# A two-layer decoder trunk on one core: layer 1's weighted sums of values as three fp32r passes instead of one fp32 matmul

## The chip, the cores and the metric

The kernel runs on one core of a Trainium2 chip. The metric is the device time of one execution in microseconds. The core has a matmul engine (TensorE, PE in the profile; its weight loads are PEld), a vector engine (VectorE, DVE), a scalar engine (ScalarE, ACT), GpSimd (POOL) and an engine that issues transfers (SyncE, SP). The engines run side by side, each through its own instructions in order, and wait for each other on semaphores.

## The reference

A sequence of 256 tokens of width 2048 goes through two layers. Each has a mixer and a squared-ReLU MLP, with RMS norms around both. Layer 0's mixer is a gated unit beside a dilated attention. Layer 1's mixer, which the change touches, is stick-breaking attention with 16 heads of 128:

```python
def block(args):
    qblk, start = args
    z = jnp.einsum('bhqe,bhke->bhqk', qblk, k).astype(jnp.float32)
    qpos = start + jnp.arange(ATT_BLOCK)
    causal = kpos[None, :] < qpos[:, None]
    log_1m_beta = jnp.where(causal, jax.nn.log_sigmoid(-z), 0.0)
    rev = lax.cumsum(log_1m_beta, axis=3, reverse=True)
    excl = jnp.concatenate([rev[..., 1:], jnp.zeros_like(rev[..., :1])], axis=-1)
    a = jnp.where(causal, jnp.exp(jax.nn.log_sigmoid(z) + excl), 0.0)
    return jnp.einsum('bhqk,bhke->bhqe', a.astype(v.dtype), v)
```

The last line, the weighted sum of the values, is what the change computes in another way.

## The kernel before

All large products are projections of 256 tokens by weights that stream in from memory. A *unit* is one projection of 256 tokens to 512 columns over a depth of 2048. It is cut into 8 *ticks*. A tick covers a depth of 256, so 2 blocks of 128, for 2 blocks of 128 tokens. To keep fp32 accuracy at the rate of fp32r, each fp32 operand is split into a high part (rounded to fp32r) and a low part (the rest), and a tick makes three matmuls for each block: high by high, high by low and low by high, 12 matmuls of 512 columns in all (`tick_tokens`).

The weights of a tick are split just in time. ACT writes `w_hi` (`conv`, L381) and DVE subtracts to get `w_lo` (`conv`, L711). A ring of four ticks holds them, so ACT may write the slot of tick t + 4 once PE has finished tick t. On ACT and DVE the work for tick t + 4 is issued at step t (`conv_at`).

Everything else is hung on these steps as `extras`, a table from a step number to a list of functions. On ACT and DVE the functions of step t are issued ahead of the split of tick t + 4. On PE they are issued ahead of the matmuls of tick t. What is issued where is therefore written out by hand, and on each engine it is done in that order.

Layer 1's input projection is done in four groups of four heads, 3 units (24 ticks) each: q, k and v (`qkv_group`). The attention of group g runs in the extras of the 24 ticks of group g + 1 (`l1_extras`), and that of the last group in the extras of the output projection (`out_phase`, whose ticks are counted the same way). For one group the old order is:

- PE: scores at step 0, the suffix sums of heads 0 and 1 at step 8 and of heads 2 and 3 at step 12 (`l1_suffix`), the values at step 15 (`l1_values`).
- ACT: logarithms at 1 and 3, high part of the softplus at 4 and 9 (`l1_soft_hi`, L538), the exponential that gives the weights at 10 and 13 (`l1_weights`, L543), high part of the output at 15 (`o_hi`, L516).
- DVE: softplus at 3 and 6, its low part at 6 and 10 (`l1_soft_lo`, L937), the exponent at 9 and 12 (`l1_exponent`, L932), low part of the output at 15 (`o_lo`, L911). DVE also turns q and k from token-major to head-major in 32x32 blocks (`turn`, L818): q at steps 9 to 14 with 2, 2, 4, 2, 4, 2 instructions (`TURNS_L1`), k at steps 17 to 20 with 4 each. The output phase has no such turns.

For one head, `values` computes 256 output columns from the first 128 keys and 128 more from the second 128 keys, both as plain fp32 matmuls:

```python
mm(ps[:, 6 + b, i * T:(i + 1) * T], v_sb[:, 0, vh], w[:, i, 0:T], i == 0, False)
last = mm(ps[:, 6 + b, i * T + P:(i + 1) * T], v_sb[:, 1, vh], w[:, i, T:TRI], False, True)
```

In the output phase the ticks that use the output of the last four heads are the ones at positions 18 and 19 (and later ones), and PE waits there for the low parts of these heads (`ready` in `out_phase`, on `s_olo`).

Of the kernel before, what the change touches and what calls it, by code (L numbers as in the profile page):

```python
# [29 lines left out]
F32 = mybir.dt.float32  # L30
F32R = mybir.dt.float32r
ALU = mybir.AluOpType
ACT = mybir.ActivationFunctionType
AX = mybir.AxisListType

P = 128
T = 256
TB = T // P
D = 2048
KT = D // P  # L40
# [13 lines left out]
HG = 4  # L54
# [5 lines left out]
TRI = 3 * P  # L60
# [40 lines left out]
def trunk_kernel(nc, x_in, pre_mix, post_mix, pre_ffn, post_ffn, ab_w_in, ln_g, ln_b, sgu_w, sgu_b,  # L101
                 ab_w_out, sb_w_in, sb_w_out, ffn_w1, ffn_w2, shapes, out):
    ctx = ExitStack()
    with ctx:  # L104
        def sb(name, shape, dt=F32):
            return ctx.enter_context(nc.sbuf_tensor(name, shape, dt))

        def sem(name):
            return ctx.enter_context(nc.semaphore(name))
# [4 lines left out]
        hid_hi = sb("hid_hi", [P, KT, T], F32R)  # L114
        hid_lo = sb("hid_lo", [P, KT, T], F32R)
# [8 lines left out]
        v_sb = sb("v_sb", [P, TB, NC])  # L124
        soft_hi = sb("soft_hi", [P, 2, TRI], F32R)
        soft_lo = sb("soft_lo", [P, 2, TRI], F32R)
        sum_mats = sb("sum_mats", [P, 2 * P], F32R)
        zs = sb("zs", [P, HG, TRI])
# [12 lines left out]
        ps = ctx.enter_context(nc.psum_tensor("ps", [P, 8, 512], F32))  # L141
# [11 lines left out]
        gain_rows = tmp[0:4 * KT, HG - 1, 0:P]  # L153
        q_flat, k_flat = (t[:, :, :].rearrange("p h t -> p (h t)").rearrange("p (b n) -> p b n", b=TB)
                          for t in (qT, kT))
        relu_tok, sq_tok, sq_T = q_flat, k_flat, qT
        q_tok, k_tok = k_flat, y_sb[:, 0, 0:T * HG].rearrange("p (b n) -> p b n", b=TB)
        junk = tmp[:, 0:HG, :].rearrange("p h c -> p (h c)")
# [52 lines left out]

        s_mix, s_sgt, s_gate, s_ghi, s_glo = (sem(n) for n in ("s_mix", "s_sgt", "s_gate", "s_ghi", "s_glo"))
        s_turned = sem("s_turned")
        s_sc = sem("s_sc")
        s_zs = sem("s_zs")
        s_sm = sem("s_sm")
# [11 lines left out]
        s_a = sem("s_a")  # L228
        s_o = sem("s_o")
# [141 lines left out]
        def _(act):  # L371
# [142 lines left out]
            def o_hi(n, b, tile):  # L514
                act.wait_ge(s_o, n + 1)
                nc.scalar.activation(hid_hi[:, bass.ds(tile, 2), :],  # L516
                                     ps[:, 6 + b, :].rearrange("p (h t) -> p h t", t=T), ACT.Copy).then_inc(s_ohi, 1)
# [6 lines left out]
            def l1_logs(b, grp):  # L524
                pair = 2 * grp + b
                z, t = zs[:, 2 * b:2 * b + 2, :], tmp[:, 2 * b:2 * b + 2, :]
                act.wait_ge(s_zs, 4 * grp + (L0_HEADS + 2 * b + 2))
                nc.scalar.activation(t, z, ACT.Abs).then_inc(s_ab, 1)
                act.wait_ge(s_ab, 3 * pair + 1)
                nc.scalar.activation(t, t, ACT.Exp, scale=-1.0).then_inc(s_ab, 1)  # L530
                act.wait_ge(s_ab, 3 * pair + 2)
                nc.scalar.activation(t, t, ACT.Ln, bias=1.0).then_inc(s_ab, 1)

            def l1_soft_hi(b, grp):
                act.wait_ge(s_sp, 2 * grp + (b + 1))
                if b == 1:
                    act.wait_ge(s_S, 2 * grp + 1)
                nc.scalar.activation(soft_hi[:, :, :], tmp[:, 2 * b:2 * b + 2, :], ACT.Copy).then_inc(s_sphi, 1)  # L538

            def l1_weights(b, grp):  # L540
                z = zs[:, 2 * b:2 * b + 2, :]
                act.wait_ge(s_e, 2 * grp + (b + 1))
                nc.scalar.activation(z, z, ACT.Exp).then_inc(s_a, 1)  # L543

            def l1_extras(grp):
                return {1: [lambda: l1_logs(0, grp)], 3: [lambda: l1_logs(1, grp)], 4: [lambda: l1_soft_hi(0, grp)],
                        9: [lambda: l1_soft_hi(1, grp)], 10: [lambda: l1_weights(0, grp)],
                        13: [lambda: l1_weights(1, grp)],
                        15: [lambda: o_hi(2 * grp + 4, 0, 4 * grp), lambda: o_hi(2 * grp + 5, 1, 4 * grp + 2)]}

            def qkv_group(u, extras):
                for i in range(3):
# [138 lines left out]
            for g in range(1, L1_GROUPS):  # L691
                qkv_group(U_IN1 + 3 * g, l1_extras(g - 1))
            out_phase(U_OUT1, l1_extras(L1_GROUPS - 1), 3)
            ffn(U_FFN1, 1)


        @block.vector
        def _(dve):
# [210 lines left out]
            def o_lo(n, b, tile):  # L909
                dve.wait_ge(s_ohi, n + 1)  # L910
                nc.vector.tensor_tensor(hid_lo[:, bass.ds(tile, 2), :], ps[:, 6 + b, :].rearrange("p (h t) -> p h t", t=T),  # L911
                                        hid_hi[:, bass.ds(tile, 2), :].bitcast(F32), ALU.subtract).then_inc(s_olo, 1)
# [11 lines left out]
            def l1_softplus(b, grp):  # L924
                dve.wait_ge(s_ab, 6 * grp + 3 * b + 3)
                t = tmp[:, 2 * b:2 * b + 2, :]
                nc.vector.scalar_tensor_tensor(t, zs[:, 2 * b:2 * b + 2, :], 0.0, t, ALU.max, ALU.add).then_inc(s_sp, 1)

            def l1_exponent(b, grp):
                dve.wait_ge(s_S, 2 * grp + (b + 1))  # L930
                for z, sums in ((zs[:, 2 * b:2 * b + 2, 0:T], ps[:, 6, :]), (zs[:, 2 * b:2 * b + 2, T:TRI], ps[:, 7, 0:T])):
                    last = nc.vector.tensor_tensor(z, z, sums.rearrange("p (h t) -> p h t", h=2), ALU.add)  # L932
                last.then_inc(s_e, 1)

            def l1_soft_lo(b, grp):
                dve.wait_ge(s_sphi, 2 * grp + (b + 1))
                nc.vector.tensor_tensor(soft_lo[:, :, :], tmp[:, 2 * b:2 * b + 2, :], soft_hi[:, :, :].bitcast(F32), ALU.subtract  # L937
                                        ).then_inc(s_splo, 1)

            def l1_extras(grp):  # L940
                return {3: [lambda: l1_softplus(0, grp)], 6: [lambda: l1_softplus(1, grp), lambda: l1_soft_lo(0, grp)],
                        9: [lambda: l1_exponent(0, grp)], 10: [lambda: l1_soft_lo(1, grp)],
                        12: [lambda: l1_exponent(1, grp)],
                        15: [lambda: o_lo(2 * grp + 4, 0, 4 * grp), lambda: o_lo(2 * grp + 5, 1, 4 * grp + 2)]}

            def qkv_group(u, extras, q_plan, scores):
                def scaled(i, dst, factor=None):
# [132 lines left out]
            for i in range(2):  # L1080
                last = nc.vector.tensor_scalar(act_hi[:, i, :], ps[:, X_BANK[0], i * T:(i + 1) * T], gpre[:, i:i + 1], None,  # L1081
                                               ALU.mult)
# [76 lines left out]
        def _(pe):  # L1159
            def mm(dst, lhsT, rhs, start, stop):  # L1160
                return nc.tensor.matmul(dst, lhsT, rhs, start=start, stop=stop, skip_group_check=True)  # L1161
# [230 lines left out]
            def values(b, w):  # L1392

                for i in range(2):
                    vh = slice((2 * b + i) * P, (2 * b + i + 1) * P)
                    mm(ps[:, 6 + b, i * T:(i + 1) * T], v_sb[:, 0, vh], w[:, i, 0:T], i == 0, False)
                    last = mm(ps[:, 6 + b, i * T + P:(i + 1) * T], v_sb[:, 1, vh], w[:, i, T:TRI], False, True)
                last.then_inc(s_o, 1)
# [9 lines left out]
            def l1_scores(grp):  # L1408

                pe.wait_ge(s_turned, grp + 3)  # L1410
                pe.wait_ge(s_olo, 2 * grp + 4)
                for h in range(HG):
                    mm(ps[:, 4 + h, 0:T], kT[:, h, 0:P], qT[:, h, :], True, True)
                    mm(ps[:, 4 + h, T:TRI], kT[:, h, P:T], qT[:, h, P:T], True, True).then_inc(s_sc, 1)

            def l1_suffix(b, grp):

                pe.wait_ge(s_splo, 2 * grp + (b + 1))
                pe.wait_ge(s_sums, 1)
                pe.wait_ge(s_zs, 4 * grp + (L0_HEADS + 4))  # L1420
                if b == 1:
                    pe.wait_ge(s_e, 2 * grp + 1)
                early = ps[:, 6, :]
                early_q1 = early.rearrange("p (h t) -> p h t", h=2)[:, :, P:T]
                late = ps[:, 7, 0:T]
                suffix_r, ones_r = sum_mats[:, 0:P], sum_mats[:, P:2 * P]
                for z, first in ((soft_hi, True), (soft_lo, False)):
                    mm(early, suffix_r, z[:, :, 0:T], first, False)
                    mm(early_q1, ones_r, z[:, :, T:TRI], False, not first)
                    last = mm(late, suffix_r, z[:, :, T:TRI], first, not first)  # L1430
                last.then_inc(s_S, 1)

            def l1_values(grp):
                pe.wait_ge(s_a, 2 * grp + 2)
                for b in range(2):
                    values(b, zs[:, 2 * b:2 * b + 2, :])

            def l1_extras(grp):
                return {0: [lambda: l1_scores(grp)], 8: [lambda: l1_suffix(0, grp)], 12: [lambda: l1_suffix(1, grp)],
                        15: [lambda: l1_values(grp)]}  # L1440

            def qkv_group(u, extras, fresh=None):
                for i in range(3):
# [130 lines left out]
```

## Time and profile before

| | |
|---|---|
| time, median of 3 runs | 2127.61 us (2127.42 to 2128.24) |
| the profiled execution | 2127.44 us, span of its trace 2125.6 us |
| TensorE clock granted over the span | 0.999 of full speed |
| PE busy | 2114.7 us, 99% |
| DVE busy | 1474.8 us, 69% |
| ACT busy | 1029.1 us, 48% |
| DMA | 406.81 MB, queue q1 at 58.0% of 16 engines' span |

A busy share is the time in which an engine had an instruction under way, over the whole span. It is an average over stages with different limits. Layer 1's attention lies between 1052 and 1415 us. There a tick takes 2.72 us when nothing else is on PE, which is the distance between ACT's splits of weights.

### The profile page before, as it was taken

The numbers are of one execution on the slowest core, as the hardware profiler recorded it, in microseconds if no ns is written. First come the engines' busy times: TensorE is split into PE (matmuls) and PEld (weight loads), VectorE is DVE, ScalarE is ACT, GpSimd is POOL, SyncE is SP. The second block draws the span as 40 slices with busy tenths as digits, with TensorE's granted clock in tenths as the row PEclk, the third lists the DMA queues.
The fourth block names the chain that finished last, engine by engine and source line by source line (L and its number), as shares of the span: only waits on it lengthen the run. The fifth ranks groups of instructions, "written<-read, shape, count | busy, mean of one in ns | idle before, by whom it ended". The sixth has DMA issues, their size and how long they took to land.

```text
span 2125.6 us, 25468 instructions
## 1 busy us (share of the span) xinstructions
PE 2114.7 (99%) x9470; PEld 1751.6 (82%) x9470; DVE 1474.8 (69%) x1902; ACT 1029.1 (48%) x1183; POOL 18.3 (1%) x24
## 2 busy tenths in 40 slices
PE   9999999999999999999999999999999999999998
PEld 7888888888888888888888888888888888888886
DVE  5797857864775775686778778577756856764875
ACT  6444445543543453454645554665434534544543
POOL 0000000000000000000000000000000000000000
PEclk9999999999999999999999999999999999999999
DMA  9655555656655656655555555456556566656553
GB/s 321 208 177 167 192 197 160 204 193 195 198 194 187 186 205 214 183 197 198 174 183 178 178 172 204 160 159 217 195 187 193 180 212 181 198 196 217 179 200 117
DMA packets 204077, 406.81 MB, mean 191 GB/s; under 512 B 6544, under 2 KB 9936, under 8 KB 203472
## 3 DMA queue, kind: packets, MB, share of 16 engines
q1 hardware_dynamic: 203856, 405.50, 58.0%
q8 instruction: 63, 1.03, 0.2%
q14 instruction: 30, 0.25, 0.0%
q10 hardware_dynamic: 128, 0.03, 0.0%
HBM read 403.41 MB, written 2.10 MB: 191 GB/s over the span
## 4 chain that ended last, share of the span: by engine, by line
PE 99%; DVE 1%; issue 0%; POOL 0%; ACT 0%; POOLq 0%; DVEq 0%
PE ps L1161 98%; PE ps L1304 1%; DVE x_sb L755 0%; PE ps L1388 0%; DVE tmp L1044 0%; POOL rst L351 0%; ACT tmp L483 0%; PE ps L1509 0%; DVE w_lo L711 0%; POOLq L104 0%; DVE act_pair L1081 0%; DVE act_pair L761 0%; DVE y_sb L1051 0%; DVEq L104 0%; DVE w_lo L789 0%
## 5 line engine op out<-in xcount | busy, mean ns | idle before, releaser
L711 DVE TENSOR_TENSOR w_lo<-w_raw,w_hi 128x1024 fp32r<-128x1024 f32 x750 | 910.4, 1225 | 573.2 <-ACT w_hi L381 570.1
L381 ACT ACTIVATE w_hi<-w_raw 128x1024 fp32r<-128x1024 f32 x750 | 789.0, 1060 | 898.2 <-PE ps L1161 894.1
L1161 PE MATMUL ps<-w_hi,act_pair 128*128 128x512 f32 x3456 | 1072.5, 390 | 0.7 <-DVE act_pair L1081 0.6
L1161 PEld LDWEIGHTS ps<-w_hi,act_pair 128*128 128x128 f32 x3456 | 647.2, 188 | 136.8 <-issue 2.2
L1161 PE MATMUL ps<-w_lo,act_pair 128*128 128x512 f32 x1728 | 670.3, 390 | 0.0
L1161 PE MATMUL ps<-w_hi,hid_hi 128*128 128x512 f32 x1280 | 498.8, 390 | 0.0
L1161 PE MATMUL ps<-w_hi,hid_lo 128*128 128x512 f32 x1280 | 498.1, 389 | 0.0
L1161 PE MATMUL ps<-w_lo,hid_hi 128*128 128x512 f32 x1280 | 498.0, 389 | 0.0
L1161 PEld LDWEIGHTS ps<-w_lo,act_pair 128*128 128x128 f32 x1728 | 324.1, 188 | 66.3 <-DVE w_lo L789 0.3
L818 DVE STREAM_TRANSPOSE qT<-kT 32x256 f32<-32x256 f32 x608 | 265.0, 436 | 42.0 <-ACT kT L593 32.7
L1161 PEld LDWEIGHTS ps<-w_lo,hid_hi 128*128 128x128 f32 x1280 | 240.3, 188 | 49.7
L1161 PEld LDWEIGHTS ps<-w_hi,hid_lo 128*128 128x128 f32 x1280 | 240.3, 188 | 49.7
L1161 PEld LDWEIGHTS ps<-w_hi,hid_hi 128*128 128x128 f32 x1280 | 240.3, 188 | 49.6
L598 ACT ACTIVATE hid_hi<-qT 128x512 fp32r<-128x512 f32 x64 | 36.9, 625 | 123.8 <-DVE qT L818 123.8
L818 DVE STREAM_TRANSPOSE kT<-y_sb 32x256 f32<-32x256 f32 x96 | 41.8, 436 | 1.6
L1009 DVE TENSOR_TENSOR hid_lo<-qT,hid_hi 128x512 fp32r<-128x512 f32 x64 | 41.2, 685 | 0.0
L589 ACT ACTIVATE qT<-ps,rst 128x512 f32<-128x512 f32 x64 | 40.0, 675 | 0.0
L593 ACT ACTIVATE kT<-qT 128x1024 f32<-128x1024 f32 x32 | 33.9, 1060 | 1.0
L412 ACT ACTIVATE act_pair<-ps,gpre 128x256 fp32r<-128x256 f32 (+1 forms) x80 | 28.7, 448 | 9.7 <-PE ps L1304 9.7
L761 DVE SCALAR_TENSOR_TENSOR act_pair<-ps,gpre,act_pair 128x256 fp32r<-128x256 f32 (+1 forms) x70 | 28.7, 456 | 2.7 <-ACT act_pair L412 2.5
L1023 DVE TENSOR_TENSOR y_sb<-y_sb,ps 128x1024 f32<-128x1024 f32 x24 | 29.2, 1216 | 0.0
L351 POOL TENSOR_TENSOR rst<-rst,neg_half 128x1 f32<-128x1 f32 (+1 forms) x13 | 9.4, 719 | 2100.2 <-DVE rst L845 2004.9
(104 smaller groups left out, 460.0 us busy)
## 6 DMA issues: line engine op xcount, KB each, us to landing
w_raw<-in_ffn_w_dram SPq DMA_DIRECT2D x256, 1024.0 KB, 5.3
w_raw<-in_sb_w_in_dram SPq DMA_DIRECT2D x48, 1024.0 KB, 5.1
w_raw<-in_ab_w_in_dram SPq DMA_DIRECT2D x36, 1024.0 KB, 5.1
w_raw<-in_ab_w_out_dram SPq DMA_DIRECT2D x16, 1024.0 KB, 5.0
w_raw<-in_sb_w_out_dram SPq DMA_DIRECT2D x16, 1024.0 KB, 5.0
w_raw<-in_ab_w_in_dram SPq DMA_DIRECT2D x6, 512.0 KB, 8.8
x_sb<-in_x_dram SPq DMA_DIRECT2D x8, 256.0 KB, 7.4
gpost<-in_norm_post_mix_dram SPq DMA_DIRECT2D x2, 1024.0 KB, 7.5
```

The costliest lines, as they stand in the source:

```text
L381: nc.scalar.activation(w_hi[:, t % RING, :, :], w_raw[:, t // 2, h:h + 2, :], ACT.Copy).then_inc(hi_ready, 1)
L412: last = nc.scalar.activation(act_hi[:, kt, part], ps[:, X_BANK[j], i * T + part.start:i * T + part.stop], ACT.Copy, scale=gpre[:, k * KT ...
L589: last = nc.scalar.activation(relu_tok[:, b, :], ps[:, 2 * (j % 2) + b, :], ACT.Relu, scale=rst[:, 6 + b:7 + b])
L593: nc.scalar.activation(sq_tok, relu_tok, ACT.Square).then_inc(f_sq, 1)
L598: nc.scalar.activation(hid_hi[:, 4 * j + i:4 * j + i + 2, :], sq_T[:, i:i + 2, :], ACT.Copy).then_inc(f_hi, 1)
L711: nc.vector.tensor_tensor(w_lo[:, t % RING, :, :], w_raw[:, t // 2, h:h + 2, :], w_hi[:, t % RING, :, :].bitcast(F32), ALU.subtract).then_ ...
L761: last = nc.vector.scalar_tensor_tensor(act_lo[:, kt, part], ps[:, X_BANK[j], i * T + part.start:i * T + part.stop], gpre[:, k * KT + kt:k ...
L818: last = nc.vector.transpose(cols[:, :, :, tp, :], rows[:, :, :, fq, :])
L1009: nc.vector.tensor_tensor(hid_lo[:, tiles, :], sq_T[:, i:i + 2, :], hid_hi[:, tiles, :].bitcast(F32), ALU.subtract).then_inc(done, 1)
L1023: nc.vector.tensor_tensor(ys, ys, bank2(j % 2), ALU.add).then_inc(post_done, 1)
L1161: return nc.tensor.matmul(dst, lhsT, rhs, start=start, stop=stop, skip_group_check=True)
L1304: last = nc.tensor.transpose(ps[:, X_BANK[j], i * T + b * P:i * T + (b + 1) * P], x_sb[:, b, kt * P:(kt + 1) * P], ident)
```

## The change

Layer 1's `l1_values` no longer calls `values`. The 256 columns over the first 128 keys become three fp32r matmuls (v high by weights high, v high by weights low, v low by weights high), and the 128 columns over the second 128 keys stay one fp32 matmul. For this ACT writes the high part of the weights (512 columns for each two heads, right behind the exponential) and of v (512 columns for four heads), and DVE the low parts. The buffers are ones that are free then: the last four tiles of `hid_hi` and `hid_lo` for the weights, `soft_hi` and `soft_lo` for v. PE's values move from step 15 to 16 and wait for the low parts. `o_hi` and `o_lo` move from step 15 to 17. DVE's new steps are 13 (low part of the first two heads' weights) and 15 (of the other two's, and v's). Layer 0 keeps `values`.

```diff
@@ -541,12 +549,17 @@
                 act.wait_ge(s_e, 2 * grp + (b + 1))
                 nc.scalar.activation(z, z, ACT.Exp).then_inc(s_a, 1)
+                act.wait_ge(s_a, 2 * grp + (b + 1))
+                nc.scalar.activation(wide_hi[:, 2 * b:2 * b + 2, :], z[:, :, 0:T], ACT.Copy).then_inc(s_a_hi, 1)
+
+            def l1_v_high(grp):
+                nc.scalar.activation(half_hi, v_first, ACT.Copy).then_inc(s_v_hi, 1)
 
             def l1_extras(grp):
                 return {1: [lambda: l1_logs(0, grp)], 3: [lambda: l1_logs(1, grp)], 4: [lambda: l1_soft_hi(0, grp)],
                         9: [lambda: l1_soft_hi(1, grp)], 10: [lambda: l1_weights(0, grp)],
-                        13: [lambda: l1_weights(1, grp)],
-                        15: [lambda: o_hi(2 * grp + 4, 0, 4 * grp), lambda: o_hi(2 * grp + 5, 1, 4 * grp + 2)]}
+                        13: [lambda: l1_weights(1, grp)], 14: [lambda: l1_v_high(grp)],
+                        17: [lambda: o_hi(2 * grp + 4, 0, 4 * grp), lambda: o_hi(2 * grp + 5, 1, 4 * grp + 2)]}
@@ -937,11 +950,21 @@
+            def l1_weights_low(b, grp):
+                dve.wait_ge(s_a_hi, 2 * grp + (b + 1))
+                nc.vector.tensor_tensor(wide_lo[:, 2 * b:2 * b + 2, :], zs[:, 2 * b:2 * b + 2, 0:T],
+                                        wide_hi[:, 2 * b:2 * b + 2, :].bitcast(F32), ALU.subtract).then_inc(s_a_lo, 1)
+
+            def l1_v_low(grp):
+                dve.wait_ge(s_v_hi, grp + 1)
+                nc.vector.tensor_tensor(half_lo, v_first, half_hi.bitcast(F32), ALU.subtract).then_inc(s_v_lo, 1)
+
             def l1_extras(grp):
                 return {3: [lambda: l1_softplus(0, grp)], 6: [lambda: l1_softplus(1, grp), lambda: l1_soft_lo(0, grp)],
                         9: [lambda: l1_exponent(0, grp)], 10: [lambda: l1_soft_lo(1, grp)],
-                        12: [lambda: l1_exponent(1, grp)],
-                        15: [lambda: o_lo(2 * grp + 4, 0, 4 * grp), lambda: o_lo(2 * grp + 5, 1, 4 * grp + 2)]}
+                        12: [lambda: l1_exponent(1, grp)], 13: [lambda: l1_weights_low(0, grp)],
+                        15: [lambda: l1_weights_low(1, grp), lambda: l1_v_low(grp)],
+                        17: [lambda: o_lo(2 * grp + 4, 0, 4 * grp), lambda: o_lo(2 * grp + 5, 1, 4 * grp + 2)]}
@@ -1432,12 +1455,21 @@
             def l1_values(grp):
                 pe.wait_ge(s_a, 2 * grp + 2)
+                pe.wait_ge(s_a_lo, 2 * grp + 2)
+                pe.wait_ge(s_v_lo, grp + 1)
                 for b in range(2):
-                    values(b, zs[:, 2 * b:2 * b + 2, :])
+                    for i in range(2):
+                        h = 2 * b + i
+                        dst = ps[:, 6 + b, i * T:(i + 1) * T]
+                        mm(dst, half_hi[:, h, :], wide_hi[:, h, :], i == 0, False)
+                        mm(dst, half_hi[:, h, :], wide_lo[:, h, :], False, False)
+                        mm(dst, half_lo[:, h, :], wide_hi[:, h, :], False, False)
+                        last = mm(dst[:, P:T], v_sb[:, 1, h * P:(h + 1) * P], zs[:, h, T:TRI], False, True)
+                    last.then_inc(s_o, 1)
 
             def l1_extras(grp):
                 return {0: [lambda: l1_scores(grp)], 8: [lambda: l1_suffix(0, grp)], 12: [lambda: l1_suffix(1, grp)],
-                        15: [lambda: l1_values(grp)]}
+                        16: [lambda: l1_values(grp)]}
```

## Rows read from the trace of the kernel before

**Rows 1.** The page: PE's share of the span, and the chain that ended last.
```profile
PE 2114.7 (99%) x9470; PEld 1751.6 (82%) x9470; DVE 1474.8 (69%) x1902; ACT 1029.1 (48%) x1183; POOL 18.3 (1%) x24
PE 99%; DVE 1%; issue 0%; POOL 0%; ACT 0%; POOLq 0%; DVEq 0%
```
**Rows 2.** The chain in order of time (start, us, what), layer 1's attention.
```profile
1052.52 362.24 PE ps L1161 x1646
```
**Rows 3.** Waits of 1050 to 1415 us: us in total, times, longest.
```profile
ACT w_hi L381 <- PE ps L1161: 161.3, 94, 4.3
```
**Rows 4.** Timeline (start, us, instruction) of PE around the first group's values.
```profile
1149.66 2.78 PE L1161 MATMUL ps<-zs,v_sb 128*128 128x256 f32 x16
1152.19 0.48 PE L1161 MATMUL ps<-w_hi,act_pair 128*128 128x512 f32 x1
1152.51 0.40 PE L1161 MATMUL ps<-w_lo,act_pair 128*128 128x512 f32 x1
```
**Rows 5.** Timeline of PE, the suffix sums in fp32r: 512, 256 and 256 columns, twice.
```profile
1140.54 0.62 PE L1161 MATMUL ps<-soft_hi,sum_mats 128*128 128x512 f32 x3
1140.99 0.64 PE L1161 MATMUL ps<-soft_lo,sum_mats 128*128 128x512 f32 x3
1141.46 0.40 PE L1161 MATMUL ps<-w_hi,act_pair 128*128 128x512 f32 x1
```
**Rows 6.** Timeline of DVE in the first group, steps 10 to 15.
```profile
1139.78 1.23 DVE L711 TENSOR_TENSOR w_lo<-w_raw,w_hi 128x1024 fp32r<-128x1024 f32 x1
...
1150.23 0.89 DVE L818 STREAM_TRANSPOSE qT<-kT 32x256 f32<-32x256 f32 x2
1151.14 1.23 DVE L711 TENSOR_TENSOR w_lo<-w_raw,w_hi 128x1024 fp32r<-128x1024 f32 x1
1152.28 1.51 DVE L911 TENSOR_TENSOR hid_lo<-ps,hid_hi 128x512 fp32r<-128x512 f32 x2
1156.36 1.23 DVE L711 TENSOR_TENSOR w_lo<-w_raw,w_hi 128x1024 fp32r<-128x1024 f32 x1 [2.57 <-ACT w_hi L381]
```
**Rows 7.** Timeline of ACT in the same stretch.
```profile
1137.73 0.85 ACT L543 ACTIVATE zs<-zs 128x768 f32<-128x768 f32 x1
1138.48 1.04 ACT L381 ACTIVATE w_hi<-w_raw 128x1024 fp32r<-128x1024 f32 x1
...
1145.44 0.83 ACT L543 ACTIVATE zs<-zs 128x768 f32<-128x768 f32 x1
1147.19 1.06 ACT L381 ACTIVATE w_hi<-w_raw 128x1024 fp32r<-128x1024 f32 x1 [0.93 <-PE ps L1161]
```
**Rows 8.** Groups of 1125 to 1197 us: count, busy us, mean ns, idle before.
```profile
L911 DVE TENSOR_TENSOR hid_lo<-ps,hid_hi 128x512 fp32r<-128x512 f32 x2 | 1.4, 688 | 0.1
L516 ACT ACTIVATE hid_hi<-ps 128x512 fp32r<-128x512 f32 x2 | 1.2, 597 | 0.9 <-PE ps L1161 0.9
```
**Rows 9.** Timeline of DVE, step 14's split in the other two groups.
```profile
1223.62 1.23 DVE L711 TENSOR_TENSOR w_lo<-w_raw,w_hi 128x1024 fp32r<-128x1024 f32 x1
1296.08 1.23 DVE L711 TENSOR_TENSOR w_lo<-w_raw,w_hi 128x1024 fp32r<-128x1024 f32 x1
```
**Rows 10.** Timeline of ACT and DVE in the output phase, splits of steps 14, 15, 16.
```profile
1367.33 1.06 ACT L381 ACTIVATE w_hi<-w_raw 128x1024 fp32r<-128x1024 f32 x1 [1.66 <-PE ps L1161]
...
1368.42 1.23 DVE L711 TENSOR_TENSOR w_lo<-w_raw,w_hi 128x1024 fp32r<-128x1024 f32 x1 [1.49 <-ACT w_hi L381]
...
1373.78 1.23 DVE L711 TENSOR_TENSOR w_lo<-w_raw,w_hi 128x1024 fp32r<-128x1024 f32 x1 [2.57 <-ACT w_hi L381]
1376.50 1.23 DVE L711 TENSOR_TENSOR w_lo<-w_raw,w_hi 128x1024 fp32r<-128x1024 f32 x1 [1.50 <-ACT w_hi L381]
```
**Rows 11.** All waits of PE in the whole execution: us in total, times, longest.
```profile
PE ps L1161 <- POOL rs_bc L337: 1.2, 1, 1.2
PE ps L1161 <- DVE act_pair L1081: 0.6, 1, 0.6
```
**Rows 12.** The first 12 us: length, PE, PEld, DVE, ACT, POOL busy, PEclk.
```profile
0.00:12.00 12.00, 10.17 (x42) 7.45 (x43) 5.03 (x10) 5.34 (x11) 0.98 (x8) 1.00 0.80 271
```

More of the change, by code:

```diff
@@ L155, in trunk_kernel @@
                           for t in (qT, kT))
+        wide_hi, wide_lo = (t[:, KT - HG:KT, :] for t in (hid_hi, hid_lo))
+        half_hi, half_lo = (t[:, :, :].rearrange("p c n -> p (c n)")[:, 0:HG * P].rearrange("p (h t) -> p h t", t=P)
+                            for t in (soft_hi, soft_lo))
+        v_first = v_sb[:, 0, :].rearrange("p (h c) -> p h c", c=P)
         relu_tok, sq_tok, sq_T = q_flat, k_flat, qT
@@ L213, in trunk_kernel @@
         s_turned = sem("s_turned")
+        s_a_hi = sem("s_a_hi")
+        s_a_lo = sem("s_a_lo")
+        s_v_hi = sem("s_v_hi")
+        s_v_lo = sem("s_v_lo")
         s_sc = sem("s_sc")
```

## The prediction

> **What bounds the kernel now.** I first read the page for the engine that is busy and on the chain that ended last. PE has 99% of both [rows 1]. So the sum of what PE does is the time, and time that ACT or DVE spend matters only where PE stands still for it. The chain in order of time then shows whether PE stands still in the stretch that is changed: it runs through layer 1's whole attention without a break, 362.24 us in one piece [rows 2]. The waits of that stretch hold none of PE on an engine; the largest, 161.3 us in 94 pieces, is ACT waiting for PE [rows 3]. Layer 1's attention is therefore hidden behind the projections today, except for its own matmuls. Two questions decide the change: how much PE time it takes off the values, and whether the new operands are ready when PE comes to ask for them. The second needs DVE's timeline, because a DVE that is 75% busy over a stretch can still be behind at the one step that matters.
>
> **The matmuls themselves.** The eight fp32 matmuls of one group of heads appear as 16 records from 1149.66 to 1152.19, 2.53 us, and the first matmul behind them takes 0.32 instead of 0.23 us, so 0.09 more [rows 4]. By columns that is 4 x (256 + 128) = 1536 columns in 2.53 us. The 256-column part is two thirds of it, 1.69 us, 0.42 each; the 128-column part 0.84, 0.21 each. The new 256-column part is 12 fp32r matmuls. No row has that mix, but the suffix sums are near: two of 512 and four of 256 columns take 1141.46 - 1140.54 = 0.92 us [rows 5]. With 2 x 0.2267 for the wide ones (a tick of 12 takes 2.72 [rows 10]) the four narrow ones take 0.47, 0.117 each. Twelve make 1.40 us against 1.69: 0.29 us less for a group of heads, 1.2 us less for four. Bounds: if each of the three new changes from fp32 back to fp32r in a group costs 0.09, as the one behind the values does today, the gain is 0.02 a group, nothing; if a 256-column pass costs just half of a 512-column one, 0.113, it is 0.33 a group, 1.3 us. I take 1.2, because the suffix sums are the same kind of instruction with changing weights.
>
> The Trainium skill (FP8 and Floating Point Precision, TensorE Precision Notes) says that true fp32 takes four passes through the array. Three passes instead of four would give back a quarter of 1.69 us, 0.42 a group and 1.7 us in all; the fp32r rows give less, and I go by them. The rule is in any case a bound on what the change can bring: under 0.1% of the run.
>
> **What ACT gets.** Two copies of 512 columns behind the exponentials and one for v, 0.60 us each [rows 8]. At step 13 the exponential ends at 1146.27 and the next split, which waits for PE, starts at 1147.19, so the copy fits in between; at step 14 ACT idles 1.66 us ahead of a split in the same rhythm [rows 10]. These two cost nothing; without that cover they would cost DVE's next split 0.6 us, as at step 10. At step 10 there is no idle time: the exponential ends at 1138.58 and its split overlaps it [rows 7]. The copy starts at about 1138.61, the split at 1139.13 instead of 1138.48 and ends at 1140.17, and DVE, which takes it up at 1139.78 today [rows 6], can do so at 1140.22. DVE is 0.45 us later.
>
> **What DVE gets, and who waits.** From 1139.78 to 1153.79 DVE has no idle time at all: its rows from step 10 to step 15 follow each other with no releaser noted, down to the first gap, 2.57 us, ahead of 1156.36 [rows 6]. So the 0.45 us of step 10 is still there at step 15. At step 13 it gets one subtraction of 512 columns. The nearest row is the output's low part, 688 ns [rows 8]; instructions that follow each other overlap by 0.09, so it adds 0.60. Queued behind it are four turns and the split of tick 17, which have slack of their own. Step 14's split started at 1151.14 and now starts at 1152.19. Step 15's two subtractions follow it, at 1153.33 and 1153.93, and end at 1154.62.
>
> PE's step 16 waits for the second one. Without the values at step 15, tick 15 starts at 1149.66 and ends 2.72 us later, at 1152.38. With some 0.05 for the semaphore PE stands still from 1152.38 to 1154.67, **2.3 us**. Nothing behind it on PE can go ahead: the whole stream is one queue. The other two groups inside the projection have the same rows, shifted by 72.5 us (step 14's split at 1223.62 and 1296.08 [rows 9]), so 3 x 2.3 = 6.9 us. Bounds for one of these: 1.7 if the copy at step 10 delays nothing and the subtractions overlap more, 2.9 if each costs its whole 0.69 and the copies on ACT 0.7.
>
> In the output phase there are no turns, and DVE keeps up: its split at step 14 runs at 1368.42, paced by ACT, which is paced by PE [rows 10]. The two subtractions start at 1369.56 and 1370.16 and end at 1370.85. Tick 15 would end at 1369.8 (ACT's 1367.33, less 0.25 from PE's last matmul to ACT, plus 2.72). PE stands 1.1 us here, even with no backlog, because a split on ACT and DVE ends 2.5 us after the tick that frees its slot, and the next tick is over after 2.72.
>
> One more wait comes from the output's move to step 17. In the output phase PE needs the low parts of the last heads at tick 18. ACT splits tick 20 after tick 16 and then makes the high part (1.06 + 0.60), DVE splits 1.23 and subtracts 0.69; with the overlaps that is 3.2 us behind the end of tick 16, and tick 17 is over after 2.72. **0.5 us**, once; between 0 and 1. The second low part has a whole tick more. In the projection groups nobody needs the output soon. The delayed o_lo does put 1.4 us ahead of k's turns at step 17, but DVE has to wait for ACT ahead of it, and by my addition its split of tick 21 ends some 6 us before PE gets there. SP reloads a quarter of the raw weights when DVE's splits have gone by; they come up to 1.1 us later for step 14, against a lead of several ticks, so no transfer becomes late. No POOL work moves.
>
> **Sum.** 6.9 + 1.1 + 0.5 - 1.2 = **+7.3 us**. The profiled execution had 2127.44 us, 1.84 more than its span, which the change doesn't touch; 2127.44 + 7.3 = 2134.7. The median of the three runs lies 0.17 above the profiled one, so 2134.9 us, 0.34% slower.
>
> **Rivals.** (a) *The operands are ready in time*, and only the passes count: 2127.6 - 1.2 = 2126.4, and by the skill's four passes 2125.9. For it: DVE is 69% busy overall and can run four ticks ahead. Against it: its splits can't run ahead, they wait for ring slots (ACT waits for PE 94 times [rows 3]), and the extras stand behind them. It holds only if step 15's subtractions end before 1152.4, when DVE's split of step 14 ends at 1152.37 even today. (b) *Half hidden*: the stops in the projection groups are under 1.2 us each, and the whole stays within 4.2 us of before: +3, 2130.6. It needs PE to be later at step 15 or DVE's delays of steps 10 and 13 to vanish (2.3 - 0.45 - 0.60 = 1.25 a stop, 3.7 + 1.6 - 1.2 = +4.1). (c) *fp32 and fp32r get in each other's way on PE*: the gain is nothing and each of the 12 narrow passes a group costs the 0.21 us of an fp32 record. 12 x 0.21 = 2.5 against 1.69, +0.8 a group instead of -0.3; +11.7, 2139.3. Against it: rows 5. (d) *The stops lower PE's clock.* PE's longest stop in the whole trace is 1.2 us, at the very start [rows 11], and the granted clock reads 1.00, 2.4 GHz, there too [rows 12]; no row has a stop of 2.3 us. If one tick after each of the three longer stops ran at 1.2 GHz, that is 3 x 2.72 = 8.2 us more, 2143.1. The Trainium skill (TensorE: Matmul & The Clock Gate, Why this matters for your kernels) warns that idle gaps between bursts throw the clock back to half; by that rule (d) is possible, and no run so far shows it.
>
> **How the numbers follow.** The forecast, that DVE's queue sets the start of the values and the stops add to about 7 us, gets 0.76; (a) 0.05; (b) 0.11; (c) 0.04; (d) 0.04. The bounds of the forecast: three stops of 1.7 to 2.9, the fourth 0.9 to 1.5, tick 18 0 to 1, the gain 1.3 to 0: from +4.7 to +11.2. They won't all fall the same way, so I take 2131.6 to 2137.2, which leaves out (a), most of (b), (c) and (d), about 2 in 10. A measurement of this kernel can tell 0.2%, 4.25 us, from no change. Slower by more is the forecast, (c) and (d): 0.84; within 0.2% is (b) and nearly all of (a), 0.15; faster by more than 0.2% has no case here, the most that the passes can give is 1.7 us, 0.01.
>
> **What would show it.** In the changed kernel's chain layer 1's attention is broken four times by DVE's subtractions at step 15, and PE's waits name them: three of about 2.3 us and one of 1.1, and a fifth of 0.5 on the output's low part. DVE's timeline runs without a gap from step 10 to step 15, with the split of step 10 taken up at 0.45 us later. The values take 2.2 to 2.3 us instead of 2.53. The prediction is wrong if PE has no wait there (then DVE had slack that I don't see), if the values take as long as before or longer, or if the ticks after a stop are slower than 2.72 us.

## The result and the profile after

The changed kernel takes 2139.05 us (median of 5 runs, 2137.15 to 2140.29) against 2127.56 us (2127.42 to 2128.24). The ratio is 1.0052 with a 95% interval of 1.0041 to 1.0064: 11.5 us slower, where 7.3 were forecast and 2137.2 us was the upper end of the range. The way it went was right, the size was not. The profiled execution took 2139.05 us with a span of 2137.2 us; its times scatter over 3.1 us, those of the kernel before over 0.8 in these five executions. A part of such scatter has nothing to do with the change: of 24 executions of the kernel before, 19 took 2127.1 to 2127.9 us and 5 took 2128.7 to 2128.9.

First the waits of 1050 to 1430 us in the changed kernel (who waited for whom, us in total, times, longest). Before, no such row had PE in front [rows 3].

```profile
PE ps L1184 <- DVE soft_lo L960: 7.7, 4, 2.2
PE ps L1184 <- DVE hid_lo L924: 0.4, 1, 0.4
```

L960 is the subtraction for v at DVE's step 15 and L924 the output's low part. These are the four stops and the fifth that the prediction named. The chain in order of time (start, us, what) shows where the first one comes from; it was one piece of 362.24 us before [rows 2].

```profile
1137.91 0.86 ACT zs L551
1138.77 0.02 issue
1138.79 0.02 ACT hid_hi L553
1138.82 0.52 issue
1139.33 1.05 ACT w_hi L389
1140.38 0.02 issue
1140.41 1.23 DVE w_lo L724
...
1147.77 0.60 DVE hid_lo L955
...
1153.59 0.60 DVE hid_lo L955
1154.19 0.61 DVE soft_lo L960
1154.81 0.14 issue
1154.94 56.71 PE ps L1184 x258
```

It is followed back from PE's first new matmul at 1154.94 through DVE's unbroken queue to the copy of step 10 on ACT (L553). The split behind that copy delays DVE's split to 1140.41; further along the chain step 13's subtraction (L955) adds 0.60. DVE's timeline of the same stretch confirms the first end: the split of step 10 now has idle time ahead of it, which it had not [rows 6].

```profile
1140.41 1.23 DVE L724 TENSOR_TENSOR w_lo<-w_raw,w_hi 128x1024 fp32r<-128x1024 f32 x1 [0.46 <-ACT w_hi L389]
```

The waits name 8.1 us of stops. From the end of the last matmul's stream it is a little more: the last one of tick 15 starts at 1304.73 and streams 0.23, PE starts again at 1307.34, so 2.38 us. Three of these, 1.20 in the output phase and 0.51 ahead of tick 18 make 8.85 us of stops. PE's timeline at the third stop, where nothing else happens:

```profile
1304.73 0.39 PE L1184 MATMUL ps<-w_hi,act_pair 128*128 128x512 f32 x1
1307.34 0.36 PE L1184 MATMUL ps<-hid_hi,soft_hi 128*128 128x256 f32 x1 [2.22 <-DVE soft_lo L960]
1307.53 0.28 PE L1184 MATMUL ps<-hid_lo,soft_hi 128*128 128x256 f32 x1
1307.65 0.28 PE L1184 MATMUL ps<-hid_hi,soft_lo 128*128 128x256 f32 x1
1307.76 0.38 PE L1184 MATMUL ps<-zs,v_sb 128*128 128x128 f32 x2
...
1309.63 0.47 PE L1184 MATMUL ps<-w_hi,act_pair 128*128 128x512 f32 x1
1309.94 0.39 PE L1184 MATMUL ps<-w_lo,act_pair 128*128 128x512 f32 x1
```

The values take 1309.63 - 1307.34 = 2.29 us here, 0.24 less than the 2.53 of before [rows 4]. Four groups give back 0.96 us. That leaves 8.85 - 0.96 = 7.9 us, and 11.5 were lost. The rest is in the same stretch of the first group:

```profile
1156.10 0.52 PE L1184 MATMUL ps<-hid_hi,soft_hi 128*128 128x256 f32 x1
1156.42 0.42 PE L1184 MATMUL ps<-hid_lo,soft_hi 128*128 128x256 f32 x1
1156.63 0.41 PE L1184 MATMUL ps<-hid_hi,soft_lo 128*128 128x256 f32 x1
...
1158.19 0.77 PE L1184 MATMUL ps<-w_hi,act_pair 128*128 128x512 f32 x1
1158.77 0.63 PE L1184 MATMUL ps<-w_lo,act_pair 128*128 128x512 f32 x1
1159.19 0.81 PE L1184 MATMUL ps<-w_hi,act_pair 128*128 128x512 f32 x2
```

The same narrow matmul follows its neighbour after 0.21 instead of 0.12 us, and a wide one after 0.42 instead of 0.23: half speed, from 1156.1 on, 1.2 us after PE had started again. In the second group it is half speed almost from the first matmul on:

```profile
1231.13 0.45 PE L1184 MATMUL ps<-hid_hi,soft_hi 128*128 128x256 f32 x1 [2.22 <-DVE soft_lo L960]
1231.38 0.42 PE L1184 MATMUL ps<-hid_lo,soft_hi 128*128 128x256 f32 x1
1231.60 0.42 PE L1184 MATMUL ps<-hid_hi,soft_lo 128*128 128x256 f32 x1
```

The views by stretch, whose sixth figure behind the length is the granted clock, agree for the stretches behind the four stops:

```profile
1154.90:1160.00 5.10, 5.06 (x25) 4.77 (x26) 2.35 (x3) 0.00 (x0) 0.00 (x0) 0.67 0.78 262
...
1231.00:1236.00 5.00, 4.87 (x24) 4.74 (x25) 2.45 (x3) 0.00 (x0) 0.00 (x0) 0.66 0.77 257
...
1307.00:1312.00 5.00, 4.67 (x30) 4.29 (x31) 2.65 (x4) 0.00 (x0) 0.00 (x0) 1.00 0.70 247
...
1381.00:1386.00 5.00, 4.98 (x32) 4.53 (x33) 1.22 (x1) 0.13 (x1) 0.00 (x0) 1.00 0.53 173
```

A mean of 0.67 over 5.10 us between the levels 1.2 and 2.4 GHz means some 3.4 us at 1.2. Such a stretch is called a fall from here on. It happened behind the first two stops of 2.4 us, not behind the third, which was as long, and not behind the one of 1.2. The values of the first group took 1158.19 - 1154.94 = 3.25 us instead of 2.29, and the two wide matmuls behind them 1.00 instead of 0.54: 1.4 us from these rows, and some 0.1 more for the rest of the tick.

### The profile page after: what moved, and what is told of

Its sections match the earlier page's. It is cut to its first block, busy times and chain, and to the rows that moved or that the text cites. A ratio compares the mean times of both kernels' runs of the same rounds, so it can differ in the third digit from the quotient of the medians.

```text
span 2137.2 us, 25528 instructions
## 1 busy us (share of the span) xinstructions
PE 2118.5 (99%) x9486; PEld 1753.8 (82%) x9486; DVE 1481.6 (69%) x1914; ACT 1035.6 (48%) x1195; POOL 18.3 (1%) x24
## 4 chain that ended last, share of the span: by engine, by line
PE 96%; DVE 3%; ACT 1%; issue 0%; POOL 0%; POOLq 0%; DVEq 0%; ACTq 0%
PE ps L1184 95%; DVE w_lo L724 1%; DVE qT L831 1%; PE ps L1327 1%; ACT w_hi L389 0%; DVE x_sb L768 0%; DVE hid_lo L955 0%; ACT L551 0%; DVE zs L945 0%; PE ps L1411 0%; ACT zs L551 0%; DVE soft_lo L960 0%; DVE tmp L1067 0%; POOL rst L359 0%; ACT tmp L491 0%
```

## The experiments

The question was whether the missing 3.6 us come from the stops (the clock falls when PE stands still) or from the new passes (narrow fp32r matmuls between fp32 ones), and whether DVE's queue is what makes the stops. Each edit is to the changed kernel.

**The values in fp32 again, everything else kept**

```diff
 def l1_values(grp):
     ...
-                    for i in range(2):
-                        h = 2 * b + i
-    ...
-                    last.then_inc(s_o, 1)
+                    values(b, zs[:, 2 * b:2 * b + 2, :])
```

> The changed kernel with one thing undone: PE computes the values as before, in fp32, while all new copies, subtractions, waits and steps stay. Two theories explain the changed kernel's 2139.05 us, which is some 3.5 us more than its stops (8.9 us) less its gain on the passes (1.0 us) give. Theory A, the stops: PE's clock falls to 1.2 GHz for a while after some of the three stops of 2.4 us, whatever PE computes behind them. Then this kernel shows the same stops, granted clock of 0.997 to 0.998 over the span, and takes about 1.0 us more than the changed one: 2138 to 2141, most likely 2139.9. Theory B, the passes: narrow fp32r passes mixed with fp32 ones lower the clock or slow PE down. Then it takes 2127.5 + 8.9 = 2136.4 and the clock reads 0.999.

Measured: 2139.37 us (2138.47 to 2141.67), ratio 1.0056 (1.0041 to 1.0072), clock 0.998. Theory B's 2136.4 is out. The waits are the same 7.7 us in 4 and 0.4 in 1, and the clock fell behind the first stop, with no fp32r pass in the values (the clock is the figure 0.89; 1.00 in the second row means that it didn't fall there):

```profile
1150.00:1165.00 15.00, 12.78 (x54) 10.51 (x53) 8.66 (x14) 3.76 (x6) 0.00 (x0) 0.89 0.45 150
...
1225.00:1240.00 15.00, 12.78 (x61) 10.55 (x60) 10.30 (x16) 5.21 (x7) 0.00 (x0) 1.00 0.59 197
```

This run also prices a fall. In its chain, the pieces of PE that begin where a stop ends and run to where the chain goes over to ACT and DVE hold the same work, one with the fall and one without:

```profile
1156.13 57.17 PE ps L1184 x254
1232.78 55.48 PE ps L1184 x254
```

The difference is 1.69 us. At that price two falls make 3.4 us in the changed kernel's profile. The fourth experiment gives 1.5 for the changed kernel's own matmuls, so 3.1 us, and 7.9 + 3.1 = 11.0 of its 11.5 us are accounted for.

**Values a step later, so that DVE is done**

```diff
-                        16: [lambda: l1_values(grp)]}
+                        17 if grp < L1_GROUPS - 1 else 16: [lambda: l1_values(grp)]}
-                        17: [lambda: o_hi(...), ...]}
+                        18 if grp < L1_GROUPS - 1 else 17: [lambda: o_hi(...), ...]}
-                        17: [lambda: o_lo(...), ...]}
+                        18 if grp < L1_GROUPS - 1 else 17: [lambda: o_lo(...), ...]}
```

> The changed kernel with PE's values of the three groups inside the projection at step 17 instead of 16, and their output parts at 18 instead of 17; the output phase stays as changed. DVE's subtractions of step 15 end 2.4 us behind the end of tick 15, and tick 16 takes 2.72 us, so the three stops should be gone and the wait be over some 0.3 us before PE asks. Theory A (stops cost their length, and the clock falls only behind them): 2127.5 - 1.0 + 1.2 + 0.5 = 2128.2 us, granted clock 0.999. Theory B (the passes lower the clock): three groups with the same passes and no stops still lose about 3.5 us, 2131.7, clock 0.997 to 0.998.

Measured: 2128.66 us (2128.37 to 2129.99), ratio 1.0007 (0.9998 to 1.0016), clock 0.999. One step takes back 10.4 of the 11.5 us, and what is left can't be told from the kernel before by the times alone. The waits keep the two of the output phase only:

```profile
PE ps L1184 <- DVE soft_lo L960: 1.0, 1, 1.0
PE ps L1184 <- DVE hid_lo L924: 0.4, 1, 0.4
```

and the chain is one piece through all three groups, with the new passes in it, up to the stop in the output phase. Theory B asked for 2131.7.

```profile
1053.94 314.17 PE ps L1184 x1444
```

**No stop at all**

```diff
 # ACT, in l1_extras
-                        13: [lambda: l1_weights(1, grp)], 14: [lambda: l1_v_high(grp)],
-                        17: [lambda: o_hi(...), ...]}
+                        13: [lambda: l1_weights(1, grp), lambda: l1_v_high(grp)],
+                        18 if grp < L1_GROUPS - 1 else 16: [lambda: o_hi(...), ...]}
 # DVE
-                        15: [lambda: l1_weights_low(1, grp), lambda: l1_v_low(grp)],
-                        17: [lambda: o_lo(...), ...]}
+                        15 if grp < L1_GROUPS - 1 else 14: [lambda: l1_weights_low(1, grp), lambda: l1_v_low(grp)],
+                        18 if grp < L1_GROUPS - 1 else 16: [lambda: o_lo(...), ...]}
 # PE
-                        16: [lambda: l1_values(grp)]}
+                        17 if grp < L1_GROUPS - 1 else 16: [lambda: l1_values(grp)]}
```

> As the one before, and the output phase rearranged: v's high part at ACT's step 13, the last two subtractions at DVE's step 14, where DVE idles 1.49 us ahead of its split, the output's high and low parts at step 16. No stop of PE is left by theory A, so only the passes count: 2127.5 - 1.0 = 2126.5 us, about 0.05% faster than the kernel before, clock 0.999. Theory B: 2130.

Measured: 2127.0 us (2126.21 to 2127.9, 11 runs) against 2127.6, ratio 0.9997 (0.9988 to 1.0007): not to be told from the kernel before. No wait of PE is left from 1050 to 1430 us, and the chain has layer 1's attention in one piece again, of 361.39 us with 1662 matmuls where it was 362.24 with 1646 [rows 2]:

```profile
1052.74 361.39 PE ps L1184 x1662
```

So the passes are worth 0.85 us by the profile, 0.04% of the run, and the times of the executions neither confirm nor deny it.

**Shorter stops: two of q's turns behind the subtractions**

```diff
-TURNS_L1 = {9: 2, 10: 2, 11: 4, 12: 2, 13: 4, 14: 2}
+TURNS_L1 = {9: 2, 10: 2, 11: 4, 12: 2, 13: 2, 14: 2, 15: 2}
```

> The changed kernel with two of the four turns of q of step 13 moved to step 15, behind the subtractions that PE waits for. They take 0.45 us each, so DVE comes to the subtractions 0.9 us earlier and each of the three stops shrinks from 2.4 to 1.5 us. If DVE's queue sets the start of the values, 2.7 us of stops go. Whether stops of 1.5 us lower the clock is open: if they don't, 2127.5 + 6.2 - 1.0 = 2132.7 us at a clock of 0.999, if they do as those of 2.4 us, about 2136 at 0.997 or 0.998. If something other than DVE's queue sets the start, the time stays at 2139.

Measured: 2133.48 us (2133.07 to 2134.43), ratio 1.0027 (1.0016 to 1.0038), clock 0.999. The stops went from 2.2 to 1.3 us in the waits, by the 0.9 of two turns, although the turns have nothing to do with the values:

```profile
PE ps L1184 <- DVE soft_lo L960: 5.0, 4, 1.3
```

and the granted clock over all four groups reads 1.00:

```profile
1100.00:1420.00 320.00, 314.67 (x1453) 261.60 (x1452) 226.62 (x300) 174.89 (x194) 0.54 (x1) 1.00 0.54 177
```

The stops got 2.7 us shorter and the time 5.6 us. The other 2.9 us are about what two falls of the clock cost, and in this profile there is none. Its chain gives their price for the changed kernel's own work. The first line below is the piece behind its first stop, without a fall. The other two are the changed kernel's pieces behind its first and second stop, each with a fall:

```profile
1155.16 55.20 PE ps L1184 x258
...
1154.94 56.71 PE ps L1184 x258
...
1231.13 56.72 PE ps L1184 x258
```

That is 1.5 us for a fall.

**ACT's copy of step 10 moved to step 12**

```diff
 def l1_weights(b, grp):
     ...
+                if b == 1:
+                    l1_weights_high(b, grp)
+            def l1_weights_high(b, grp):
+                z = zs[:, 2 * b:2 * b + 2, :]
                 act.wait_ge(s_a, 2 * grp + (b + 1))
                 nc.scalar.activation(wide_hi[:, 2 * b:2 * b + 2, :], z[:, :, 0:T], ACT.Copy).then_inc(s_a_hi, 1)
-    10: [lambda: l1_weights(0, grp)],
+    10: [lambda: l1_weights(0, grp)], 12: [lambda: l1_weights_high(0, grp)],
```

> The changed kernel with ACT's copy of the first two heads' weights moved from step 10, where ACT has no idle time, to step 12, where it idles 2.6 us; DVE needs it at 13. If this copy delays DVE's split by 0.45 us and the delay reaches step 15, as I worked out, each of the three stops is 0.45 us shorter, 1.9 to 1.95 us, and with no effect on the clock the time is 2127.5 + 7.5 - 1.0 = 2134.0 us at 0.999. If stops of 1.9 us lower the clock now and then, it is 2135 to 2137. If the copy was hidden, the stops stay at 2.2 in the waits and the time at 2139.

Measured: 2134.51 us (2134.25 to 2135.95), ratio 1.0032 (1.002 to 1.0045), clock 0.999. The stops are 1.8 us in the waits, 0.43 shorter than 2.22: the copy's delay on ACT reached PE fifteen microseconds later through DVE's queue.

```profile
PE ps L1189 <- DVE soft_lo L965: 6.4, 4, 1.8
```

**Longer stops: v's low part written three times**

```diff
+            def l1_v_low_again(grp):
+                for n in range(2 if grp < L1_GROUPS - 1 else 0):
+                    dve.wait_ge(s_v_lo, 3 * grp + (n + 1))
+                    nc.vector.tensor_tensor(half_lo, v_first, half_hi.bitcast(F32), ALU.subtract).then_inc(s_v_lo, 1)
-    15: [lambda: l1_weights_low(1, grp), lambda: l1_v_low(grp)],
+    15: [lambda: l1_weights_low(1, grp), lambda: l1_v_low(grp), lambda: l1_v_low_again(grp)],
-                pe.wait_ge(s_v_lo, grp + 1)
+                pe.wait_ge(s_v_lo, 3 * grp + (3 if grp < L1_GROUPS - 1 else 1))
```

> The changed kernel with v's low part written three times instead of once in the three groups inside the projection, one after the other, and PE waiting for the last: nothing else moves, each of the three stops grows by two subtractions of 0.65 to 0.7 us, from 2.4 to 3.7 or 3.8 us. That is 4.1 us more of plain stops. If the clock falls by a stop's length and not by what runs behind it, it falls behind every one of the three now, at about 1.7 us each, 5.1 us in all: 2127.5 + 8.9 + 4.1 - 1.0 + 5.1 = 2144.6 us, with three stretches at 1.2 GHz in the profile. If it falls by chance, as behind two of three in the changed kernel's profile, the time is 2141 to 2145 and scatters as that one's does.

Measured: 2147.66 us (2145.36 to 2148.08), ratio 1.0090 (1.0074 to 1.0107), clock 0.994. That is 3 us above the forecast. In the profile the clock fell at all three stops, as forecast, but each fall was longer (the view of 1150 to 1165 us has a mean clock of 0.77, so 6.9 us at 1.2 GHz, where the changed kernel's has 0.89 and 3.3 us). A part of it lies in the stop, where PE does nothing anyway:

```profile
1156.60:1162.00 5.40, 5.32 (x23) 5.18 (x24) 2.39 (x3) 0.00 (x0) 0.00 (x0) 0.51 0.54 176
...
1235.00:1240.00 5.00, 4.87 (x22) 4.80 (x23) 2.45 (x3) 0.00 (x0) 0.00 (x0) 0.50 0.54 161
...
1313.60:1318.00 4.40, 4.32 (x21) 4.35 (x21) 2.40 (x3) 0.00 (x0) 0.00 (x0) 0.50 0.45 141
```

PE ran at 1.2 GHz from its first matmul behind the stop until 1161.9. Its timeline has the values of the first group from 1156.68 to 1160.94, 4.26 us instead of 2.29:

```profile
1156.68 0.55 PE L1189 MATMUL ps<-hid_hi,soft_hi 128*128 128x256 f32 x1 [3.68 <-DVE soft_lo L965]
...
1160.94 0.77 PE L1189 MATMUL ps<-w_hi,act_pair 128*128 128x512 f32 x1
1161.51 0.56 PE L1189 MATMUL ps<-w_lo,act_pair 128*128 128x512 f32 x1
1161.91 0.62 PE L1189 MATMUL ps<-w_hi,act_pair 128*128 128x512 f32 x2
```

With the two wide ones (0.97 instead of 0.54) a fall costs 2.4 us. One of the four executions took 2145.36 us at a clock of 0.997, the other three 2147.6 to 2148.1 at 0.994, so its falls were fewer or shorter. The sum is then 7.9 + 3 x 1.5 for the longer stops + 3 x 2.4 = 19.6 us, and 20.1 were measured. 4.5 us more of stops cost 8.6 us.

**The output's parts at step 16 in the output phase**

```diff
-                        17: [lambda: o_hi(...), ...]}
+                        17 if grp < L1_GROUPS - 1 else 16: [lambda: o_hi(...), ...]}
-                        17: [lambda: o_lo(...), ...]}
+                        17 if grp < L1_GROUPS - 1 else 16: [lambda: o_lo(...), ...]}
```

> The changed kernel with the output's high and low parts at step 16 instead of 17 in the output phase alone. The stop ahead of tick 18 (0.35 us in the waits, 0.5 with the matmul's end) should be gone and nothing else change: 0.5 us less than the changed kernel, 2138.5 us, which its scatter hides; the profile decides, by the wait on the output's low part.

Measured: 2138.14 us (2136.31 to 2139.9), ratio 1.0046 (1.0029 to 1.0063), clock 0.997. The wait on L924 is gone from the profile and the other four stay, 7.7 us. The effect on the time is inside the scatter, as expected. The four executions show what the scatter is: 2136.3 and 2136.6 us at a clock of 0.998, 2139.7 and 2139.9 at 0.997.

## Why the prediction was right or wrong

The likeliest case was one mechanism, DVE's queue setting the start of the values, and that mechanism is shown. The time missed because the sum put nothing for the clock behind a stop: a rival that was given 4 in 100 turned out to run on top of the likeliest case.

- **The three stops inside the projection**: forecast 2.3 us each, measured 2.22 in the waits and 2.38 from the end of the last stream. Moving two unrelated turns (-0.9) and one copy (-0.43) shortened them by just what these instructions take in DVE's queue.
- **The copy at step 10**: forecast a delay of 0.45 us to DVE and a split at 1140.22; the split came at 1140.41, 0.63 us later than the 1139.78 of before [rows 6]. Of that 0.18 lies ahead of the attention: the suffix sums stand at 1140.72 where they stood at 1140.54 [rows 5]. The other 0.45 is the copy, and its removal gave 0.43. From the last subtraction to PE's first matmul the chain has 0.14 us, where 0.05 was taken.
- **The stop in the output phase**: forecast 1.1, measured 1.05 in the waits. **The stop ahead of tick 18**: forecast 0.5, measured 0.35 in the waits, 0.51 from the stream's end.
- **The passes**: forecast 1.2 us of gain, 2.2 to 2.3 us for a group's values. The values take 2.29 behind a stop (1.0 us in all), and 0.85 us is the chain's difference with no stop. Between pieces of the chain without a fall it is 0.28 a group, 55.48 us with fp32 values (first experiment) against 55.20 (fourth), so the forecast's 0.29 lies at the upper end of what was seen. The bound of the Trainium skill's four passes, 1.7 us (FP8 and Floating Point Precision, TensorE Precision Notes), was the less accurate number; the fp32r rows of the suffix sums [rows 5] were the nearer.
- **The sum** of these, +7.3, would have been +7.9 with the measured terms. The step that failed stands in rival (d): "If one tick after each of the three longer stops ran at 1.2 GHz", priced at 8.2 us with a chance of 0.04. It was set low because no row of the kernel before has a stop of PE over 1.2 us [rows 11]. That no row shows it was read as evidence against it, where it was no evidence at all. The size was off too: what ran behind the stops were two falls of 1.5 us each in the profile, and not three of 2.72. Over a quarter of the loss came from a term that the sum did not have, and the upper end of the range, 2137.2, left no room for it. The prediction did name the sign, ticks slower than 2.72 us behind a stop.
- The Trainium skill (TensorE: Matmul & The Clock Gate, Why this matters for your kernels) warned of this: idle gaps between bursts take the clock back to half. The runs agree in kind: a mean granted clock of 0.66 and 0.67 behind two stops of 2.4 us, 0.50 and 0.51 behind three of 3.8 (3.7 in the waits). They differ in length, since the page speaks of longer gaps than the 2.4 us that were enough here in some cases; the measurement decides.
- **The clock at the start was misread.** The prediction took the 1.00 of [rows 12] to mean 2.4 GHz behind the stop of 1.2 us. The chain of the kernel before has four transposes of x at 4.31 us and four of the same size at 8.37 us:

```profile
4.31 0.90 PE ps L1304 x4
...
8.37 0.44 PE ps L1304 x4
```

The first four took twice as long, as matmuls do at 1.2 GHz. In the kernel with the values a step later, four wide matmuls from 7.43 to 9.14 us follow each other after 0.43 us, the spacing at 1.2 GHz, and the clock column reads 1.00 for 6 to 12 us there as well. So the 1.00 is no evidence that PE ran at 2.4 GHz at the start. And the trace of the kernel before does show the clock falling once PE stands still for longer: PE's last matmul starts at 2116.28, the view by stretch reads 1.00 from 2119 to 2121 us and 0.50 from 2123 to 2125.6.

Rival (a), operands ready in time, was wrong for this kernel and right for the three groups of the one with the values a step later (2128.66 us, with the output phase's stops left). Rival (b) was wrong: no delay vanished. Rival (c), fp32 and fp32r in each other's way, is out by 2.29 against 2.53 us for the same four heads. That its 2139.3 us is nearly the measured 2139.05 is luck.

The times of whole executions hide a second thing. The chain reaches layer 1's attention at 1052.5 to 1053.0 us in four of the profiles (the kernel before, the changed one, no stop at all, longer stops) and at 1053.8 to 1054.0 in the other five, so some 1.1 us differ ahead of everything that was changed. From that point to PE's last long piece (1433.67 us before) the profiles have:

| kernel | us | more than before |
|---|---|---|
| before | 381.15 | |
| no stop at all | 380.31 | -0.84 |
| values a step later | 382.23 | 1.08 |
| shorter stops | 386.88 | 5.73 |
| copy at step 12 | 388.29 | 7.14 |
| output's parts at step 16 | 392.05 | 10.90 |
| fp32 values again | 392.55 | 11.40 |
| changed | 392.63 | 11.48 |
| longer stops | 401.11 | 19.96 |

The sum of stops from the stream's end, passes (-0.84) and falls (1.5 each, 2.4 behind the longer stops) falls short of these by 0.2 to 0.4 us in the kernels with stops. With fp32 values again (no gain, one fall of 1.7) it is 0.9.

What stays open: where these 0.2 to 0.9 us go, and why one stop of 2.4 us is followed by a fall and the next isn't. Where a fall lies was seen in one profile of each kernel only (two of three stops in two kernels, one of three in a third). That the number of falls spreads the changed kernel's times fits the clock of each execution, 0.998 for the two fastest (2137.15 and 2138.08 us) and 0.997 for the other three, but the falls of the executions without a profile were not seen.

## What to carry to other kernels

When the bound engine has to wait for an operand, look up where the producer stands in its own queue at that step, and not how busy it is on average: DVE was 69% busy over the span and 2.3 us late, and everything ahead of the operand in that queue counted in full, down to two turns that belong to another stage. Before a wait goes on TensorE, give it a step of slack: the same edit one step later cost 1.1 instead of 11.5 us. And price a stop of TensorE of more than 2 us at more than its length, since the work behind it may run at 1.2 GHz: here 1.5 to 2.4 us more for each fall. A clock column that reads 1.00 is worth a check against the spacing of equal matmuls.

## What was not expected of the hardware

A stop's price is not in proportion to its length. Of stops of 1.3 us in the waits (three, one profile) and 1.8 us (three, one profile) none was followed by a fall of the granted clock. Of the stops of 2.2 us in the waits one or two of three were, for some 3.4 us of which each cost 1.5 to 1.7. At the stops of 3.7 us the clock fell at all three in the profile, was down from the first matmul on, and each fall cost 2.4 us beyond the stop. Falls came behind values in fp32 (one of three stops) as behind values in fp32r (two of three). The lower clock need not begin with the stop: in the first group of the changed kernel it set in 1.2 us after PE had started again. And fp32r matmuls of 256 columns with changing weights follow each other after 0.12 us, but the first of three behind an fp32 one takes 0.19 to 0.20, so three of them against one fp32 matmul of 0.42 save less than a quarter.
